# A decoder step on Trainium2: four of six convolution tiles as phase-stored window matmuls, two ahead of the memory-query chunk and two among the attention steps

## The reference, cut to what matters

```python
proj = h @ w_in_a                                  # h = rmsnorm(x); 1024 -> 768 + 768 + 256
ga, gb, qm = split(proj, [768, 1536])
u = ga * sigmoid(gb)
u_ext = concatenate([conv_prev, u], axis=1)        # 30 rows of the past (zeros for the prompt)
c = depthwise_conv(u_ext, conv_w)  + conv_b        # 31 taps, 768 channels, every channel by itself
o_main = silu(layernorm(c, ln_g, ln_b))
o_mem = mem_attention(qm, mem_k, mem_v)            # 4 heads of 64, 256 memory tokens
mix = concatenate([o_main, o_mem]) @ w_out_a
x = x + rmsnorm(mix)
```

## Time and profile before

| | us |
|---|---|
| median of three runs | 1942.44 |
| lowest, highest | 1941.63, 1943.37 |
| the profiled execution | 1947.18 |
| its span in the profile | 1945.3 |
| PE busy in the span | 1719.2 (88%) |
| DVE busy | 980.7 (50%) |
| ACT busy | 706.1 (36%) |
| POOL busy | 591.4 (30%) |

### The profile page before, as it was taken

One profiled execution on the slowest core, in us unless ns is written; L12 is line 12 of the kernel. 1 busy time (PEld: TensorE's weight loads), 2 busy tenths in 40 slices (PEclk: granted clock), 3 DMA queues, 4 the chain that ended last, 5 costly groups with the idle time before them and its releaser, 6 DMA issues.

```text
span 1945.3 us, 28543 instructions
## 1 busy us (share of the span) xinstructions
PE 1719.2 (88%) x11088; PEld 1528.7 (79%) x11088; DVE 980.7 (50%) x1170; ACT 706.1 (36%) x864; POOL 591.4 (30%) x337
## 2 busy tenths in 40 slices
PE   3699958789999999698898998399999999999991
PEld 2698528789999999698766476398998988989881
DVE  3479863521111000513387424476676866758664
ACT  3333214322222221313255232254454544545443
POOL 0742003234555343232100021241422414224232
PEclk9799878899999999899889999599999999999996
DMA  4332201215554433121532515469697796977934
GB/s 129 109 108 98 82 0 44 66 45 150 148 152 135 154 125 102 44 87 44 199 121 75 160 55 130 164 200 242 204 295 200 238 240 212 289 195 236 258 108 159
DMA packets 347411, 282.10 MB, mean 145 GB/s; under 512 B 11719, under 2 KB 311787, under 8 KB 347337
## 3 DMA queue, kind: packets, MB, share of 16 engines
q1 hardware_dynamic: 327769, 252.28, 44.6%
q10 hardware_dynamic: 16320, 16.52, 2.5%
q0 software_dynamic: 3264, 12.50, 1.7%
HBM read 246.89 MB, written 35.09 MB: 145 GB/s over the span
## 4 chain that ended last, share of the span: by engine, by line
PE 43%; issue 26%; DVE 13%; POOL 12%; ACT 3%; DMA 2%; SPq 1%; POOLq 0%; DVEq 0%; ACTq 0%
PE ps L1844 32%; POOL ea L757 8%; DVE cT L1273 5%; POOL ea L759 1%; PE ps L1806 1%; POOL hl L668 1%; DVE rstd L1196 1%; PE ps L1796 1%; PE ps L2125 1%; PE ps L1869 1%; DVE zc L1481 1%; PE ps L2176 1%; DVE tmp L1400 1%; ACT zc L1010 1%; DMA memtok<-in_mem_prompt 1%
## 5 line engine op out<-in xcount | busy, mean ns | idle before, releaser
L2343 PE MATMUL ps<-ejx,ewh 128*128 128x384 f32 x1408 | 404.5, 361 | 3.2 <-issue 1.7
L1703 DVE TENSOR_TENSOR ewl<-eraw,ewh 128x2048 fp32r<-128x2048 f32 (+1 forms) x144 | 303.9, 2111 | 183.5 <-ACT ewh L1127 183.2
L1127 ACT ACTIVATE ewh<-eraw 128x2048 fp32r<-128x2048 f32 (+1 forms) x144 | 255.3, 1774 | 308.3 <-PE ps L2346 167.0
L2346 PE MATMUL ps<-ejx,ewl 128*128 128x192 f32 x1408 | 353.8, 251 | 0.0
L1844 PE MATMUL ps<-hh,whi 128*128 128x260 f32 x1504 | 313.4, 290 | 42.4 <-DVE hl L1391 27.5
L757 POOL TENSOR_TENSOR ea<-eat,ea 128x128 fp32r<-128x128 f32 x88 | 181.8, 2066 | 430.9 <-ACT ea L1151 430.9
L1844 PE MATMUL ps<-hh,wlo 128*128 128x260 f32 x1504 | 306.9, 286 | 0.0
L1844 PE MATMUL ps<-hl,whi 128*128 128x260 f32 x1504 | 306.8, 286 | 0.0
L661 POOL TENSOR_TENSOR wlo<-raw,whi 128x2048 fp32r<-128x2048 f32 x46 | 213.1, 4633 | 204.4 <-ACT whi L787 79.7
L1844 PEld LDWEIGHTS ps<-hh,whi 128*128 128x128 f32 x1504 | 237.8, 192 | 46.7 <-issue 30.0
L2343 PEld LDWEIGHTS ps<-ejx,ewh 128*128 128x128 f32 x1408 | 266.1, 189 | 6.5 <-issue 6.5
(11 more groups left out here) (370 smaller groups left out, 2631.5 us busy)
## 6 DMA issues: line engine op xcount, KB each, us to landing
eraw<-in_w_gate_e SPq DMA_DIRECT2D x88, 512.0 KB, 4.9
eraw<-in_w_up_e SPq DMA_DIRECT2D x88, 512.0 KB, 6.1
eraw<-in_w_down_e SPq DMA_DIRECT2D x64, 512.0 KB, 5.8
eraw<-in_w_down_e SPq DMA_DIRECT2D x48, 256.0 KB, 2.7
xs<-zero ACTq DMA_DIRECT2D x10, 1152.0 KB, 4.8
raw<-in_w_gate_d SPq DMA_DIRECT2D x22, 512.0 KB, 4.0
raw<-in_w_up_d SPq DMA_DIRECT2D x22, 512.0 KB, 5.2
raw<-in_w_down_d SPq DMA_DIRECT2D x16, 512.0 KB, 4.2
```

The lines of the kernel that those rows point to most:

```text
L1127: e.activation(ewh[:, s, 0:n], eraw[:, u % RAW, 0:n], ACT.Copy).then_inc(ew_hi, 1)
L1703: e.tensor_tensor(ewl[:, s, 0:n], eraw[:, u % RAW, 0:n], ewh[:, s, 0:n].bitcast(F32), ALU.subtract)\
L2343: e.matmul(ps[:, q, 0:2 * C], ewh[:, s, o:o + P], ejx[:, k, :, :].rearrange("p h n -> p (h n)"), start=(k == 0), stop=(k == KD - 1), skip_ ...
L2346: ins = e.matmul(ps[:, q, C:2 * C], ewl[:, s, o:o + P], ejx[:, k, 0, :], start=False, stop=(k == KD - 1), skip_group_check=True)
```

## The change

Two of the six tiles (FN = 2) stay on VectorE, with 62 taps. Four (FP = 4) go to TensorE in another form. All activations of mixer A are stored by phase: token 4t + g lies in plane g at place t (PH = 4 planes of 130, 128 for the prompt and 2 for decode). The planes come about where the normed input is split: ScalarE and GpSimd read `tmp` with a step of four elements.

For a phase tile, DMAs on SP's queue (`shift`, 16 for each tile) regroup 32 channels by 4 phases on the 128 partitions. Then one matmul multiplies a window of 4 taps of 32 channels at once. A group of 32 channels takes nine matmuls of 128 x 128 by 128 columns, 16 groups in all. Their weights (128 x 1152) are built by multiplying a column of taps with an identity of 32: the first four on VectorE ahead of the products, the others on VectorE (even) and GpSimd (odd), each when its slot of a ring of four is free. ScalarE copies the result of four groups (`conv_evict`), and 16 more DMAs (`unshift`) bring it back. The tap table for the builds is loaded early by four DMAs with pieces of 32 channels, and turned by 16 transposes ahead of the sums of the first norm.

TensorE does groups 0 to 7 between the input projection and the memory-query chunk, and groups 8 to 15 among the prompt's attention steps. The diagonal taps go. The decode part of attention takes the form of mixer B: no cache transposes, scores on VectorE, values as 16 matmuls. The layer norm's sums over tiles are added up on VectorE, so that TensorE sums one tile each time. The bias of the phase tiles is added in the partial sums and in the subtraction of the mean. The second output-weight chunk is split early: its high part on ScalarE behind head 0, its low part on GpSimd between builds 9 and 11. The output projection's results are put back in token order as they leave PSUM.

```diff
+FN = 2
+FP = FS - FN
+PH = 4
+LEAD = 8
+WIN = TP // PH + LEAD
+NW = LEAD + 1
+SUB = P // PH
+NG = FP * PH
+WSLOTS = 4
...
@@ program of SP @@
+            for s in range(PH):
+                e.dma_start(crow4[5 - s:5 - s + CW, :].rearrange("k (q s c) -> k q s c", s=PH, c=SUB)[:, :, s, :], tapw)\
+                    .then_inc(us_in, 16)
...
+            def shift(k):
+                e.wait_ge(tile_free[1], M_IN // 2 + FN + k + 1)
+                e.wait_ge(us_in, 16 * PH + 256 * k)
+                for q in range(PH):
+                    for s in range(PH):
+                        e.dma_start(ushift[SUB * s:SUB * s + SUB, k, q, :], ubp[SUB * q:SUB * q + SUB, k % 2, s, 0:WIN])\
+                            .then_inc(us_in, 16)
+            def unshift(k):
+                e.wait_ge(ce, k + 1)
+                if k:
+                    e.wait_ge(cb_in, 256 * k)
+                for q in range(PH):
+                    for b in range(PH):
+                        g = PH - 1 - b
+                        e.dma_start(cT[SUB * q:SUB * q + SUB, FN + k, g * TQ:g * TQ + TP // PH],
+                                    cP[SUB * b:SUB * b + SUB, k % 2, q * P:(q + 1) * P]).then_inc(cb_in, 16)
+            shift(0)
             e.wait_ge(w_lo, U_QM - 1)
             load_whole(U_QM % 2, win, 2 * FS * P)
...
             for i in range(2):
+                shift(1 + i)
                 e.wait_ge(w_lo, U_OUTA + i - 1)
                 load_whole((U_OUTA + i) % 2, a["w_out_a"][0], i * 2 * P)
             mem_rows(0, memA)
+            shift(3)
+            e.wait_ge(tile_done, M_OUTA)
+            mem_cache("cache_mem_k", 0, memA.kc, mc_in, range(4))
+            copied_out(e, TP_MA + 1)
+            e.dma_start(qdrA[:, :], qrowA[0:B, :]).then_inc(qd_out, 16)
+            e.wait_ge(qd_out, 16)
+            e.dma_start(memA.qb[:, :, :], row_broadcast(qdrA[0, :], [[NMEM, B], [1, NMEM]])).then_inc(qm_in, 16)
+            e.wait_ge(mc_in, 64)
+            mem_cache("cache_mem_k", 0, memA.kc, mc_in, range(4, B))
...
+            unshift(0)
+            unshift(1)
+            e.wait_ge(mb_step, B)
+            mem_cache("cache_mem_v", 0, memA.vc, mv_in)
+            unshift(2)
+            unshift(3)
...
@@ program of GpSimd @@
+                e.tensor_tensor(out=planes(hl[:, k, :]), in0=phased(tmp[:, t % NTMP, :]),
+                                in1=planes(hh[:, k, :].bitcast(F32)), op=ALU.subtract).then_inc(tmp_used, 1)
...
+            for n in range(WSLOTS + 1, NG, 2):
+                e.wait_ge(cg, n - WSLOTS + 1)
+                dst, taps, own = window_weights(n)
+                e.tensor_tensor(out=dst, in0=taps, in1=own, op=ALU.mult).then_inc(wb_pool, 1)
+                if n == NG // 2 + 1:
+                    lo_of(U_OUTA + 1)
...
@@ program of VectorE @@
-                conv_taps(8 if p < 2 else 10)
-            mem_dve(memA, qmA, T_MIXA, conv_taps, conv_decode, conv_last)
-            conv_taps(FS * CW)
+                conv_taps(13)
+            build(4)
+            conv_decode()
+            build(6)
+            build(8)
+            maxima(0)
+            build(10)
+            shares(memA, 0)
+            maxima(1)
+            turned(memA, 0)
+            shares(memA, 1)
+            e.wait_ge(qm_in, 16)
+            e.wait_ge(mc_in, 64)
+            mem_scores(memA, 0, 0)
+            mem_scores(memA, 2, 0)
+            maxima(2)
+            turned(memA, 1)
+            build(12)
+            shares(memA, 2)
+            e.wait_ge(mc_in, 16 * B)
+            mem_scores(memA, 4, 0)
+            mem_scores(memA, 6, 0)
+            maxima(3)
+            build(14)
+            turned(memA, 2)
+            shares(memA, 3)
+            decode_max(3, 0)
...
+            sum_tile(1, 0)
+            sum_tile(2, 1)
+            decode_shares(memA, 0)
+            sum_tile(3, 2)
+            decode_turned(memA, 3, 0, 1)
+            sum_tile(4, 3)
+            turned(memA, 3)
+            sum_tile(5, 4)
...
@@ program of ScalarE @@
+            weights(memA, 0)
+            weights(memA, 1)
+            turned(memA, 0)
+            hi_of(U_OUTA + 1)
+            weights(memA, 2)
+            conv_evict(2)
+            turned(memA, 1)
+            weights(memA, 3)
+            turned(memA, 2)
+            decode_weights(memA, 3, 0)
+            e.preload_act_table(ACT.Sqrt)
+            conv_evict(3)
+            turned(memA, 3)
...
@@ program of TensorE @@
+            def conv_group(*ns):
+                for n in ns:
+                    k, q = n // PH, n % PH
+                    if q == 0:
+                        e.wait_ge(us_in, 16 * PH + 256 * (k + 1))
+                        if k == FP - 1:
+                            e.wait_ge(ce, k)
+                    e.wait_ge(*built(n))
+                    for i in range(NW):
+                        ins = e.matmul(ps[:, CONV_BANK[k], q * P:(q + 1) * P], wring[:, n % WSLOTS, i * P:(i + 1) * P],
+                                       ushift[:, k, q, i:i + P], start=(i == 0), stop=(i == NW - 1), skip_group_check=True)
+                    ins.then_inc(cg, 1)
+            e.wait_ge(root_ready, 1)
+            conv_group(*range(2 * PH))
             chunk_tiles(U_QM, M_QM, 0, 0, 0)
...
+            mem_scores(memA, qmA, 0, 0)
+            conv_group(8, 9)
+            mem_scores(memA, qmA, 0, 1)
+            conv_group(10)
+            turn(memA, 0)
+            mem_values(memA, 0)
+            mem_scores(memA, qmA, 0, 2)
+            conv_group(11)
+            turn(memA, 1)
+            conv_group(12)
+            mem_values(memA, 1)
+            mem_scores(memA, qmA, 0, 3)
+            conv_group(13, 14)
+            turn(memA, 2)
+            decode_scores(memA, 3, 0)
+            conv_group(15)
+            decode_turn(memA, 3, 0)
+            mem_values(memA, 2)
+            turn(memA, 3)
+            e.wait_ge(mp_e, NT * MH)
+            e.wait_ge(ln_acc, FS - 1)
+            ln_sums(tmp[:, 2, :])
+            mem_values(memA, 3)
+            decode_values(memA, ps[0:32, 3, NMEM:2 * NMEM], 0, 16 * B)
+            e.wait_ge(ln_mean, 1)
+            e.wait_ge(ln_used, FS - 1)
+            ln_sums(tmp[:, 3, :])
+            decode_pick(memA, 3, 0)
```

More of the change, by code:

```diff
@@ L1234, in _ @@
             norm_tiles(T_N0, x, G_PRE_MIX)
+            for n in range(2):
+                f = TP_W + n
+                copy_out(f, wcol[:, 8 * n:8 * n + 8, :].rearrange("p q k -> p (q k)"), ps[:, bank(f), 0:8 * NW * PH])
             for n in range(8):
@@ L1247, in _, with build @@
                 ins.then_inc(tp_free[f % 2], 1)
+            def build(n):
+                if n >= WSLOTS:
+                    e.wait_ge(cg, n - WSLOTS + 1)
+                dst, taps_, own = window_weights(n)
+                e.tensor_tensor(out=dst, in0=taps_, in1=own, op=ALU.mult).then_inc(wb_dve, 1)
+            e.wait_ge(sel_ready, 5)
+            copied_out(e, TP_W)
+            copied_out(e, TP_W + 1)
+            for n in range(WSLOTS):
+                build(n)
             def tap_order():
-                left = [0] * (FS - 1)
-                for n in range(8):
+                left = [0] * FN
+                for n in range(13):
                     yield 0, n
@@ L1256, in tap_order @@
                 while min(left) < CW:
-                    for f in [f for f in range(FS - 1) if left[f] < CW][:2]:
+                    for f in [f for f in range(FN) if left[f] < CW]:
                         yield f, left[f]
@@ L1361, in _ @@
+            e.wait_ge(u_zero, 3)
             for p in range(FS):
@@ L1569, in _ @@
+            turned(memB, MH + 1)
+            maxima(MH + 3)
+            decode_shares(memB, MB_ALL)
+            mix_low(FS, ps[:, 6, :], MIX_ALL + FS + 1)
             e.wait_ge(sd_pv, B)
@@ new lines, in decode_turn, with decode_values @@
+            def decode_turn(m, q, done):
+                e.wait_ge(mb_step, done + MB_P)
+                for i in range(MT):
+                    ins = e.transpose(ps[:, q, 32 * i:32 * i + 32], m.pd[:, i * P:(i + 1) * P], ident[0:32, 0:32])
+                ins.then_inc(mb_step, 1)
+            def decode_values(m, dst, done, landed):
+                e.wait_ge(mb_step, done + MB_PT)
+                e.wait_ge(mv_in, landed)
+                for b in range(B):
+                    for i in range(MT):
+                        ins = e.matmul(dst, m.pdp[:, i, 32 * b:32 * b + 32], m.vc[:, b, i, :],
+                                       start=(b == 0 and i == 0), stop=(b == B - 1 and i == MT - 1))
+                ins.then_inc(mb_step, 1)
@@ new lines, in _, with ln_sums @@
+            for t in range(2):
+                e.wait_ge(tile_free[t], M_OUTA // 2)
+            fill(TP_MA + 1, [(ps[0:B, 5, c * P:(c + 1) * P], qmA[:, c, TP:T]) for c in range(FM)])
+            copied_out(e, TP_MA)
+            def ln_sums(src):
+                for h in range(2):
```

(4 more changed lines are left out.)

760 lines of the change are left out of this document (354 added, 406 removed).

## The result

The changed kernel takes 1966.16 us (median of 4 runs, 1965.62 to 1967.83), the kernel before 1942.04 us beside it: a ratio of 1.0117, 95% interval 1.0105 to 1.013. That is 22.7 us slower by the ratio and 24.1 by the two medians. The time is 31.5 us above the forecast of 1934.7, outside its range. The profiled execution took 1965.62 us (span 1963.8).

A forecast was written before the change was run, and what follows sets the result against it. VectorE's convolution taps were taken to bound the kernel up to mixer A's layer norm root. Terms +33.9, -45.7, tail +0.3, early +1.8 and +2 gave -7.7 us: 1934.7 against the median 1942.44, range 1920 to 1954.

The forecast's parts named there:

- I cost them at nothing: Early part: the tap table's four DMAs should land before TensorE asks, at no cost; if late, the sums wait one for one.
- +1.8: Early part: sixteen short transposes of the tap table ahead of the pre-norm sums add 1.8 us to the chain.
- rival C: Early part: GpSimd's strided reads cost 8 us instead of 2, or the table lands as late; no change, 1941; chance 0.20.
- I take 0.38: Shifts and unshifts on SP's queue: each small DMA issue takes 0.38 us, between bounds 0.30 and 0.65; 6.1 us a tile.
- The landing: Shifts and unshifts: a move's data lands 2.8 us after issue; the last unshift, issued by 270.6, lands at 273.4.
- the account of VectorE blocked by GpSimd: Input projection: taps, copies and five GpSimd splits of 4.6 us sum to 71.6 us on VectorE up to the sixth product.
- a wait of 2.8 us at each chunk: Input projection: TensorE waits about 2.8 us for VectorE's product at each chunk from the second on; projection 12 us later.
- Groups: Convolution on TensorE: nine fp32 matmuls of 128 columns take 2.2 us if load and columns overlap, 4.0 if not.
- Group 6: Ahead of the memory-query chunk: waits for weights VectorE builds, held by GpSimd's split and builds, until 194.8 us.
- group 11's wait: In attention: GpSimd's low part of the second output weight stands ahead of build 11, a new wait of 7 us.
- the low parts: Pre-norm: GpSimd's eight low parts read with a step of four elements, costing +2 us, 14.8 instead of 12.8.
- D: Attention: TensorE works at the low clock, 0.50, putting the first output-projection tile 17.6 us later; slower, 1952 us; chance 0.25.

The follow-up runs named there:

- e9: Changed kernel with each of the tap table's four 31-row DMAs split into 16 and 15 rows, transposes still ahead of the sums; ratio 1.0014 to the kernel before.
- e3: Changed kernel with the third unshift issued ahead of the eight cache loads and the last unshift shared between SP and ScalarE; ratio 1.0058 to the kernel before.
- e4: Changed kernel with nine instead of thirteen taps behind each input-projection product, the other seventeen behind build 8; ratio 1.0046 to the kernel before.
- e6: Changed kernel with GpSimd's two output-weight splits moved later, behind builds 5 and 7 and behind the attention; ratio 1.0023 to the kernel before.
- e1: Changed kernel with the tap table's sixteen transposes moved behind the pre-norm sums; ratio 1.0018 to the kernel before.
- e2: Changed kernel with the tap table's four DMAs issued ahead of the memory weight loads, transposes still ahead of the sums; ratio 1.0046 to the kernel before.
- e5: Changed kernel with the tap table loaded as four DMAs of 31 whole 2 KB rows and reordered by a GpSimd copy; ratio 1.0084 to the kernel before.
- e7: Changed kernel with the changes of e1, e3, e4 and e6 together; 1916.03 us beside 1945.94 for the kernel before, ratio 0.9842.
- e10: e7 plus the tap table's DMAs in 16 and 15 rows and half the third unshift issued by GpSimd; 1913.14 us beside 1945.62, ratio 0.9833.
- e8: The kernel before, unchanged, traced a second time; span 1941.7 us instead of 1945.3, first output-projection tile ending at 315.69.

## Why the prediction was wrong

**What fell: "The DMAs queue behind small loads on SP and should land before TensorE asks; I cost them at nothing."** The early part was 17.2 of the 31.5 us, and this step some 16 of them: TensorE waited 15.2 for the table, and e9, which puts only the table right, starts the projection 16.3 earlier. The sums took 10.1 us instead of 7.4, at a granted clock of 0.72 from 49 to 60 us (before the change 1.00). By e9 most of that comes with the transposes in front of them and not with the wait: transposes and sums together took 3.1 us more there than the sums alone had before, where I had +1.8. I had written that the sums wait one for one if the table is late, and priced that in rival C, but with 6 us (from -7.7 to -1.7) and without a row for a DMA of 31 rows. A transfer without a row deserved bounds like the others. The trace of before had a warning in the same place of SP's queue, the issue of a load of 4 KB:

```profile
20.42 2.83 SPq L429 DMA_DIRECT2D br<-in_b_router  x1
```

Whatever held it, four more issues at that price would have ended at 34.6, an estimate, with the landing still to come, where TensorE began the sums at 34.0: by this row the table could not be taken to be in time. The Trainium skill has the rule that I did not weigh (DMA: Bandwidth & Descriptors, Why a DMA increments its semaphore by 16 and not by 1): a DMA runs on the largest number of engines up to 16 that divides the slowest dimension of both sides, and that is 1 for 31 rows. This case agrees: 31 rows gave 14 GB/s with small pieces, and 25 with large ones at a DMA share of 0.06, one engine of 16; 16 and 15 rows with the same pieces had an issue of 0.46 us.

**What was mis-sized: "I take 0.38" for an issue of a move.** It is 0.67 in a row of sixteen, just above my upper bound of 0.65. That costs twice: unshift 2 takes 4.7 us more, so that the last unshift starts 4.3 later, and that one then takes 10.8 us instead of 6.1. The landing was 1.8 instead of 2.8. Together 8.0 us, where the last partial sum was 7.5 late; e3 took 7.9 back. From there to the first tile 0.8 more.

So the 31.5 us are 17.2 in the early part, 8.3 from there to the first tile and 5.9 behind it.

**What the middle's steps did, by their numbers.** Taps: 62 as forecast, 60 of them at L1404, with the maximum near 5 us again:

```profile
L1404 DVE SCALAR_TENSOR_TENSOR cT<-ubn,cwT,cT x60: 737/747/5097, 130.8 to 197.4; 128x512 f32<-128x512 f32 x60
```

The projection ended 81.1 us behind its start, forecast 81.3, and VectorE's work from the first to the sixth product took 69.5 us against 71.6: the account of VectorE blocked by GpSimd held, also in e4 and e6. How that reached TensorE was other than forecast: not a wait of 2.8 us at each chunk but two waits, 3.5 and 4.3, with slower pairs behind each, so that the close match of the total is in part luck. Groups at 2.04 against 2.2. Group 6 started at 214.9 (forecast, shifted by the late start, 215.8), and group 11's wait was 6.0 against 7. The first head's scores took 3.78 us at a granted clock of 0.50 (236.2 to 240.0), behind waits of 2.0 and 0.5 for ScalarE, against 1.99. Group 15 ended 2.6 us later than forecast, hidden behind the queue of moves. The transposes cost 1.9 (1.8 forecast), the low parts 1.85 (2 forecast).

The shortest of those low parts on GpSimd took 1557 ns against 1286 before, 1.21 times. The rule of the Trainium skill weighed in the prediction (GPSIMD Engine Reference, Performance pitfalls for Q7 kernels), half again, was more than this trace shows.

**The rivals.** C named the right mechanism (the table late), with too small a price; D had the right sign by the wrong mechanism: the clock in the attention was 0.79 from 236 to 292, not 0.50, and the groups in it took 2.2 to 3.3 us each, but for one of 4.2 (group 11, at 0.50 behind its wait). So the sign came out as in D for a reason that I had capped in C. Undoing C's mechanism alone (e1, e9) leaves the kernel 0.1 to 0.2% above the one before, where a gain of 7.7 us should have stood; that is the second error, the moves (8.3 to the first tile), and what stays open behind that tile.

**What stays open** are the 6 us behind the first tile. For 2.9 of them the place is known: from the first tile to the start of the last pair of down-projection matmuls the kernel before took 470.0 us and the changed one 472.9, as e1, e2, e5 and e9 did (472.9 to 473.0), while e3, e4, e6, e7 and e10 took 470.3 to 470.8, with the same instructions. The windows at the same place, 86 to 96 us behind the first tile (busy us of PE, PEld, DVE, ACT and POOL, granted clock, DMA share, GB/s), first before:

```profile
401.70:411.70 10.00, 8.82 (x63) 8.85 (x64) 3.01 (x5) 3.72 (x4) 5.91 (x2) 0.83 0.01 2
```

then after:

```profile
419.60:429.60 10.00, 8.62 (x49) 8.65 (x50) 2.50 (x4) 3.07 (x3) 5.88 (x2) 0.66 0.01 2
```

TensorE gets through 63 instructions in one and 49 in the other, behind the same root and reciprocal. In the same window e8, e3, e4, e6, e7 and e10 have 0.83 again, and e1, e2, e5 and e9 0.66, so it seems to go with the kernel and not with the execution, though only the kernel before was traced twice. Why the clock returned sooner in one than in the other wasn't tried.

## What to carry to other kernels

Look at the row count of every new DMA and at what waits for it, above all for small tables loaded at the start: four loads of 62 KB held SP's queue for 19.5 us here, and both cures, splitting them by rows and asking for them later, showed no price of their own. Count small moves by the issuing queue's own pace (here 0.67 us each in a row) and by what else stands in that queue. When VectorE gives work away, put what is left of it where VectorE was idle, and GpSimd's long subtractions where VectorE has nothing to do; here these orders decided whether the same convolution lost 1.2% or gained 1.6%.

## What was not expected of the hardware

- A DMA of 31 rows moved 14 GB/s in pieces of 128 bytes and 25 GB/s in rows of 2 KB, the latter with one sixteenth of the DMA engines' time in use. In the small pieces each issue held SP's queue for 4.6 us; in 16 and 15 rows of the same pieces an issue took 0.46 us.
- SP and ScalarE issued a move of 32 pieces of 512 bytes every 0.62 to 0.68 us, GpSimd one every 0.52.
- One copy of 16 elements from SBUF to SBUF on VectorE took 4.50 us beside a GpSimd subtraction and 0.17 without it, so the block isn't confined to taps, which read two tiles.
- The sums of the first norm took 7.5 us at a granted clock of 1.00 with nothing new in front, and 9.3 at 0.82 with sixteen transposes from 36 partitions in front of them and 0.28 us of idle time.
- The same matmuls behind the same root and reciprocal got a granted clock of 0.83 or 0.66 in the same 10 us; the whole stretch of 2016 of them took 243.74 us in the one and 245.19 in the other.
